# A hybrid decoder step: the end of the sliding-window attention woven differently into the last tile of the RWKV recurrence

## What is computed

```python
def step(S, inp):                                    # RWKV-7, per token and head
    r_t, w_t, k_t, v_t, a_t, b_t = inp
    sa = jnp.einsum('bhij,bhj->bhi', S, a_t)
    S = S * w_t[:, :, None, :] + sa[..., None] * b_t[:, :, None, :] + v_t[..., None] * k_t[:, :, None, :]
    return S, jnp.einsum('bhij,bhj->bhi', S, r_t)

def swa_banded(q, k, v, sink):                       # blocks of 128 queries against 256 keys
    ...
    s = jnp.einsum('bnqkgd,bnskd->bnkgqs', qb, kc.astype(F32)) * (Dh ** -0.5)
    s = jnp.where(valid[None, :, None, None], s, -jnp.inf)
    pr = sink_softmax(s, sink)
    o = jnp.einsum('bnkgqs,bnskd->bnqkgd', pr.astype(v.dtype), vc)
    return o.reshape(B, T, Hq * Dh)
```

## Time and profile before

| | |
|---|---|
| three timed runs | 837.72 us median (835.63 to 838.18) |
| the profiled execution | 839.23 us, its span in the trace 837.4 us |
| TensorE busy | 702.7 us (84%) |
| VectorE busy | 371.4 us (44%) |
| ScalarE busy | 214.9 us (26%) |
| granted TensorE clock, mean over the span | 0.894 of full speed |

### The profile page before, as it was taken

How to read it: one execution, slowest core, us unless ns; L and a number is a source line. 1 busy time by engine, 2 the same in 40 slices (tenths; PEclk the granted TensorE clock), 3 DMA queues, 4 the chain that set the end, 5 groups by cost and what they waited for, 6 DMA issues and landing times.

```text
span 837.4 us, 16076 instructions
## 1 busy us (share of the span) xinstructions
PE 702.7 (84%) x6956; PEld 530.7 (63%) x6956; DVE 371.4 (44%) x740; ACT 214.9 (26%) x538; POOL 92.4 (11%) x122
## 2 busy tenths in 40 slices
PE   3999999999979898667997989877699269999933
PEld 3874887878878888556753448655246257777711
DVE  4210129993365575645483330354325742222216
ACT  4250115334222222434501110322112002222214
POOL 0100000000765000000000000000000024344210
PEclk9999999999999999957988998975789569999966
DMA  9622340002101000320407011023608849999725
GB/s 309 245 101 100 101 139 13 1 1 59 61 4 54 3 4 4 114 47 2 180 28 270 31 56 45 1 79 96 209 25 327 354 144 377 409 405 405 307 93 237
DMA packets 42492, 113.90 MB, mean 136 GB/s; under 512 B 10187, under 2 KB 12677, under 8 KB 41116
## 3 DMA queue, kind: packets, MB, share of 16 engines
q1 hardware_dynamic: 36964, 102.18, 33.2%
q0 software_dynamic: 4864, 8.53, 2.9%
q10 hardware_dynamic: 592, 2.13, 0.7%
HBM read 105.88 MB, written 16.24 MB: 146 GB/s over the span
## 4 chain that ended last, share of the span: by engine, by line
PE 70%; DVE 18%; ACT 5%; issue 4%; DMA 2%; SPq 0%; POOL 0%; POOLq 0%; DVEq 0%; ACTq 0%
PE bank L874 51%; PE bank L1494 7%; PE bank L878 5%; PE bank L1508 4%; PE bank L1480 2%; DVE arena L1918 1%; PE bank L1502 1%; ACT arena L1667 1%; DMA arena<-pair_d 1%; DVE arena L2100 1%; DVE arena L1963 1%; DVE arena L2032 1%; ACT arena L1684 1%; DVE arena L1990 1%; DMA arena<-hn_d,arena 1%
## 5 line engine op out<-in xcount | busy, mean ns | idle before, releaser
L874 PE MATMUL bank<-arena 64*64 64x64 f32 (+11 forms) x5156 | 527.4, 296 | 60.2 <-DMA arena<-pair_d 11.8
L874 PEld LDWEIGHTS bank<-arena 64*64 64x64 f32 (+5 forms) x5156 | 392.4, 158 | 183.9 <-issue 102.7
L878 PE MATMUL bank<-arena 128*128 128x128 f32 (+4 forms) x392 | 58.2, 301 | 50.9 <-issue 16.6
L878 PEld LDWEIGHTS bank<-arena 128*128 128x128 f32 (+4 forms) x392 | 50.3, 167 | 66.1 <-issue 27.9
L1494 PEld LDWEIGHTS bank<-arena 128*64 128x64 f32 x1024 | 58.6, 138 | 19.7 <-issue 19.7
L830 POOL DMA_INDIRECT arena<-hn_d,arena x16 | 16.7, 1044 | 434.3 <-DVE arena L2299 412.1
L1494 PE MATMUL bank<-arena 128*64 128x128 f32 x1024 | 63.5, 276 | 0.0
L2320 DVE TENSOR_TENSOR arena<-bank,arena 128x512 f32<-128x512 f32 x32 | 22.1, 692 | 54.5 <-PE bank L1480 54.5
L1599 ACT COPY arena<-bank 128x260 f32<-128x260 f32 x40 | 15.0, 375 | 108.1 <-PE bank L874 108.1
L834 POOL DMA_INDIRECT pair_d<-arena x32 | 31.8, 993 | 61.1 <-ACT arena L1801 54.1
L1699 ACT COPY arena<-bank 128x256 f32<-128x256 f32 x56 | 20.8, 372 | 63.8 <-PE bank L874 62.3
(11 more groups left out here) (238 smaller groups left out, 550.2 us busy)
## 6 DMA issues: line engine op xcount, KB each, us to landing
arena<-in_w_exp_gate SPq DMA_DIRECT2D x32, 512.0 KB, 10.9
arena<-in_w_exp_up SPq DMA_DIRECT2D x32, 512.0 KB, 13.2
arena<-in_w_exp_down SPq DMA_DIRECT2D x32, 512.0 KB, 14.2
arena<-in_w_in SPq DMA_DIRECT2D x5, 2048.0 KB, 9.5
arena<-in_x_prompt SPq DMA_DIRECT2D x8, 512.0 KB, 6.2
arena<-in_w_out SPq DMA_DIRECT2D x2, 2048.0 KB, 10.9
arena<-in_cache_mem_k SPq DMA_DIRECT2D x8, 512.0 KB, 7.5
arena<-in_cache_mem_v SPq DMA_DIRECT2D x8, 512.0 KB, 3.8
```

The lines of the kernel that those rows point to most:

```text
L874: last[0] = pe.matmul(out, lhsT, rhs, start=start, stop=stop, skip_group_check=True)
L878: last[0] = pe.transpose(out, in_, ident[0:n, 0:n])
```

## The change

The order of the steps behind `fin` of tile 3 is another, and `wp` is two steps now: `wt` (normalise, transposes, their copies) and `wv` (products with the values, the copy of the outputs). Nothing is added to or taken from the work of an engine.

```diff
-RECUR_ORDER += [("ws", 1, 0), ("U", 3, 0), ("wp", 0, 0), ("S", 3, 0), ("ws", 2, 0), ("U", 3, 1), ("wp", 1, 0),
-                ("S", 3, 1), ("ws", 3, 0), ("Y", 3, 0), ("wp", 2, 0), ("wp", 3, 0)]
+RECUR_ORDER += [("U", 3, 0), ("ws", 1, 0), ("S", 3, 0), ("wt", 0, 0), ("U", 3, 1), ("ws", 2, 0), ("wv", 0, 0),
+                ("S", 3, 1), ("wt", 1, 0), ("Y", 3, 0), ("ws", 3, 0), ("wv", 1, 0), ("wt", 2, 0), ("wv", 2, 0),
+                ("wt", 3, 0), ("wv", 3, 0)]
...
-                  "wp": [(("pT", t, i), "a") for i in range(4)] + [(("o", t), "a")]}[what]
+                  "wt": [(("pT", t, i), "a") for i in range(4)],
+                  "wv": [(("o", t), "a")]}[what]
...
-            def window_outputs(t, _):
-                done(pe, ("vtok",))
+            def window_weights_T(t, _):
                 pe.wait_ge(s_prob, t + 1)
                 na = 1 if t == 0 else 2
                 sm = SmW[t % 2].rearrange("p (h s) -> p h s", h=H)
...
                             tr(o[:, (2 * n + a) * P:(2 * n + a + 1) * P], sm[:, 2 * i + n, a * P:(a + 1) * P])
                     close()
+
+            def window_outputs(t, _):
+                na = 1 if t == 0 else 2
+                done(pe, ("vtok",))
                 done(pe, ("pT", t, 3))
                 o = reuse(pe, ("o", t))
                 for h in range(H):
...
-                elif what == "wp":
+                elif what == "wt":
                     na = 1 if t == 0 else 2
                     for i in range(4):
                         o = filled(act, ("pT", t, i))
                         act.copy(PTa[:, 2 * i:2 * i + 2, 0:na, :],
                                  o[:, :].rearrange("p (n a q) -> p n a q", n=2, a=2)[:, :, 0:na, :]) \
                             .then_inc(evac["a"], 1)
+                elif what == "wv":
                     o = filled(act, ("o", t))
...
-                elif what == "wp":
+                elif what == "wt":
                     normalise(t, P, H, P if t == 0 else 2 * P, sinks)
```

More of the change, by code:

```diff
@@ L1216, in _ @@
             steps = {"rq": rotated_query, "rk": rotated_key, "vk": window_values, "ws": window_scores,
-                     "wp": window_outputs, "sample": lambda *_: None,
+                     "wt": window_weights_T, "wv": window_outputs, "sample": lambda *_: None,
                      "tok": by_token, "AB": chunk_products, "N0": first_N, "level": level, "fin": last_products,
```

## The result

The changed kernel takes 829.59 us (median of 20 runs, 825.0 to 839.91) against 837.95 us for the kernel before (20 runs beside it, 833.31 to 844.06). The ratio is 0.9897, 95% interval 0.9875 to 0.9918: faster by 8.4 us, where 4.0 us were forecast. All ratios here leave out executions that took over 1.5% longer than the fastest of their kernel, such as the one of 839.91 us.

A forecast was written before the change was run, and what follows sets the result against it. Bound: a loop through TensorE, VectorE and ScalarE from 343 to 404 us, with TensorE idle and its clock falling. An early loss, then gains, left about 4.0 us: 837.72 − 4.0 = 833.7 us, range 829.5 to 839.5.

The forecast's parts named there:

- Wait for `WT`: Ahead of `U` (3,0): TensorE waits about 1.1 us for ScalarE's copies, tile 1's scores begin later, loss 1.8 us.
- First loop: Tile 1's scores to tile 0's transposes: these move from 354.45 to 355.6 us, 1.1 us later; clock falls in 4.6 us idle.
- Second loop at 0.50: Tile 0's transposes to tile 1's, at half clock: the latter begin at 371.2 against 374.19 us, 3.0 us earlier.
- Third loop: Tile 1's transposes, then `Y`: clock returns inside `Y`, scores of tile 3 begin near 377.9 and not near 383.4 us.
- Rival C: Clock doesn't return before the scores of tile 3: only 1 to 2 us earlier, 836.2 us; chance 0.16.
- Fourth loop: Scores of tile 3 to transposes of tile 2: these begin at 387.5 against 393.03 us, 5.5 us earlier.
- The tail: End of the list, up to 404.04 us: 5.5 or 2.0 us earlier depending on the clock; middle taken, about 4.0 us.
- the lower end: Clock not back for tile 2's products with the values: they cost 1.8, tile 3's transposes up to 1.7 more; 2.0 us earlier.
- Behind 404 us: After the list: `wkvT`, `ysT` and the loads of `w_out` move earlier too, so 839.23 − 4.0 = 835.2 us profiled.
- B: Clock doesn't fall in the first new idle time: 11.4 us faster, 826.3 us; chance 0.06.
- D: Clock stays at 0.50 to the end of the list: 3.5 us later, 841.2 us; chance 0.08.
- E: The order does nothing net, tile 1's normalisation ending as late as before: 837.7 us; chance 0.08.

The follow-up runs named there:

- u_late: Changed kernel with the first two steps exchanged, `U` (3,0) again behind the scores of tile 1: median 831.39 us, ratio to before 0.9917.
- warm_half: Changed kernel with 18 identity products ahead of each of the first three waits for normalised weights: median 825.04 us, ratio to before 0.9848.
- norm_first: Changed kernel with VectorE's normalisations of tiles 1 and 2 moved ahead of the next tile's evictions: median 828.81 us, ratio to before 0.9893.

## Why the prediction was right in the stretch and wrong behind it

1. *Wait for `WT`*: right. 1.11 us, ended by ScalarE's copies. That something is lost by it, net, was never shown; in u_late the exchange is worth 1.5 us up to the second transposes and 0.2 us at the third.
2. *First loop*: right. Transposes at 359.61 − 4.2 = 355.4, forecast 355.6; idle time 4.75 us, forecast 4.6; the clock fell in it.
3. *Second loop at 0.50*: right. 375.18 − 4.2 = 371.0, forecast 371.2, and VectorE was what TensorE waited for.
4. *Third loop*: right. The clock came back inside `Y`, at about 381.1 − 4.2 = 376.9, and the scores of tile 3 ran at 1.00, from 382.40 − 4.2 = 378.2 on, forecast 377.9. The return inside `Y` was a choice that no row forced, so it was partly luck. Rival C, which the Trainium skill (TensorE: Matmul & The Clock Gate, Part 4: PE-mode transpose) spoke for, did not come; at 391.4 to 394.8 us, where TensorE ran nothing but transposes, the clock went from 0.50 to 1.00, against that page, as in before.
5. *Fourth loop*: right. 391.93 − 4.2 = 387.7, forecast 387.5.
6. *The tail*: a term of the wrong size, 4.0 us where the stretch gained 5.4. The good branch came: tile 3's products ended at 402.85 − 4.2 = 398.7, forecast 398.5 for it. I had taken 4.0, the middle of 5.5 and 2.0 us. And the lower end was too low: in u_late the clock stayed down there, and the price was 1.7 us on the products, with the transposes of tile 3 at 1.97 us as before, not 3.5 us. With that the lower end is 3.8 us. Between the first two traces the gain is 5.4 us; against the mean of three traces of before, whose own clock varies there, it is 4.6 us.
7. *Behind 404 us*: this step failed. It took for granted that a microsecond won before 404 us reaches the end, and put any change of the part behind at nothing, without a row for it. The loads of `w_out` did move earlier with the handover (issued at 406.81 against 408.01 us): the first 35 us behind it take the same time in both kernels (VectorE's last step ahead of the output products starts 1.2 us earlier in after, as the handover does). But the part behind as a whole took 429.9 us in the mean of three traces of before and 425.2 us in those of after, **4.7 us less for the same instructions**. About 3 us of them repeat in every trace, in cross-attention and just ahead of it, where the clock falls and returns at other places once the handover comes a few tenths of a us sooner or later; the rest varies from trace to trace. b_one and a_two, which add one and two products ahead of the handover to before and after and change nothing else, show in one trace each that this moment decides where the clock is down in cross-attention.

So by the traces 4.6 us come from the stretch and 4.7 us from the part behind, while the part ahead, which the change doesn't touch, happened to be 3.0 us longer in the three traces of after (mean 348.5 against 345.5 us); the spans differ by 6.2 us. The medians, over more executions, say 8.4 us, and how these divide was not measured. About half of what the two parts win is therefore not the doing of the waits that the order was made for. That it went the same way as the forecast was luck: with two products of 0.23 us put ahead of the handover most of the whole gain is gone (a_two).

Rivals: B did not come but its price was about right (warm_half); D's condition, a clock that stays down, did not occur; E fell with steps 3 to 5.

What stays open: the median of b_one shows less than its trace, that of a_two more, and only one execution of each was profiled. Why the last 225 us take 1 to 4 us less in the traces of after is not shown. What share of the executions of a kernel falls into which of the patterns behind the handover was not measured. Nor was it tried whether norm_first with another handover gains the 5 us that its trace leaves behind it.

## What to carry to other kernels

Follow the queue of the engine that a stall waits for, step by step with measured durations: here the new schedule came out to a few tenths of a us as long as the clock went as assumed. A wait for copies is worth splitting from what stands behind it; here the split and the order paid only together. Do not take it for granted that work behind the change keeps its duration: where the clock goes up and down, its parts may differ by 1 to 2% with the moment at which they begin (424.8 to 432.4 us here for the same instructions in before and after), so a gain of that size should be checked with a delay of a few tenths of a us put behind the change, in both kernels. Where TensorE stands idle for 4 to 5 us ahead of much work, filling the wait with products that nobody needs may win more than reordering does, so long as they end about when the wait does: here the stretch went from 55.1 to 48.3 us with 18 and to 57.0 us with 36.

## What the hardware showed that I had not expected

- The same 2390 matrix instructions behind the handover took 423.0 to 432.4 us over 16 traces, sorted by the moment of the first fall of the clock: 430.2 to 430.9 us in the four with 14.46 to 14.65 us, 424.2 to 426.1 us in the eight with 14.80 to 15.10 us, 428.3 to 432.4 us in the three with 15.15 to 15.22 us (all of before), 423.0 us in the one with 16.49 us. One identity product more moved the kernel before from the third of these groups to the second.
- 18 products of 128x128, 4.1 to 4.3 us in each of three waits, kept the clock at 1.00 over a stretch of 48.3 us, which took 55.1 us in after with 27.3 us of them at 0.50.
- 16 transposes in fp32 brought the clock back in after (391.9 to 395.2 us) and not in u_late (388.4 to 392.1 us), with the same products and the same 4.60 us of idle time ahead of them. In after the clock had fallen 0.6 us ahead of the transposes, at 391.35 us, in u_late 2.3 us ahead of them, at 386.10 us.
